# The accumulator of the fetched value rows in SBUF instead of two PSUM banks

## What is computed

```python
q = (xt @ w_query).reshape(t, 8, 2, 128)
s = einsum('thpd,hpkd->thpk', q, sub_keys)       # product keys
# top-16 per half, then top-16 of the 16 x 16 sums, for 8 heads:
# experts es (t, 128) out of 16384 and their softmax gates gs (t, 128)
u = expert_u[es]
vv = expert_v[es]                                # rows of 1024
a = gelu(einsum('tkd,td->tk', u, xs))
y = einsum('tk,tkd->td', gs * a, vv)
x = layer_norm(ALPHA * x + ga2 * y, ln2_g, ln2_b)
```

## Time and profile before

| | |
|---|---|
| median of 3 runs | 2309.18 us (2309.13 to 2312.66) |
| the profiled execution | 2312.7 us |
| its span | 2310.9 us |
| PE busy | 1959.6 us (85%) |
| DVE busy | 1613.4 us (70%) |
| POOL busy | 971.7 us (42%) |
| ACT busy | 196.6 us (9%) |
| DMA | 669.14 MB, mean 290 GB/s |

### The profile page before, as it was taken

The page is one execution under the profiler, slowest core; times in us unless marked ns, Lnnn a source line. Parts: engine busy times, 40 slices in busy tenths (PEclk is TensorE's granted clock), DMA queues, the critical chain, the costliest instruction groups (busy, mean ns, idle before and its releaser), DMA issues.

```text
span 2310.9 us, 22648 instructions
## 1 busy us (share of the span) xinstructions
PE 1959.6 (85%) x8018; PEld 1343.0 (58%) x8018; DVE 1613.4 (70%) x2879; ACT 196.6 (9%) x370; POOL 971.7 (42%) x1051
## 2 busy tenths in 40 slices
PE   3878799878899688999999999899999766999900
PEld 0557644355444247998889964347878766444400
DVE  0210476699678787899995897556565599776698
ACT  0020010134200001111100000000000000000000
POOL 7000026655455540145551026565555255655462
PEclk8889899967899898999997579999999755899955
DMA  9898648977799984269994039999999465899994
GB/s 290 301 319 250 236 138 310 314 246 237 267 372 332 365 309 175 73 229 347 338 359 149 1 145 363 356 409 409 409 410 409 153 216 188 336 409 409 410 410 184
DMA packets 227588, 669.14 MB, mean 290 GB/s; under 512 B 20476, under 2 KB 46204, under 8 KB 227356
## 3 DMA queue, kind: packets, MB, share of 16 engines
q0 software_dynamic: 114240, 410.27, 47.8%
q1 hardware_dynamic: 109504, 245.39, 29.4%
q10 hardware_dynamic: 3744, 12.14, 1.5%
HBM read 658.23 MB, written 7.39 MB: 288 GB/s over the span
## 4 chain that ended last, share of the span: by engine, by line
PE 44%; DVE 21%; DMA 17%; issue 12%; POOL 6%; ACT 0%; POOLq 0%; DVEq 0%; SPq 0%
PE psum L702 19%; PE psum L734 9%; DMA arena<-in_expert_v_dram,arena 9%; DVE psum L1381 7%; POOL arena L493 5%; DVE arena L1169 5%; PE psum L816 5%; PE psum L722 5%; DMA arena<-in_expert_u_dram,arena 3%; PE psum L573 2%; DMA arena<-in_w_ada_dram 2%; DMA arena<-in_w_in_dram 1%; DVE arena L1153 1%; DVE arena L1422 1%; DVE arena L1416 1%
## 5 line engine op out<-in xcount | busy, mean ns | idle before, releaser
L1169 DVE CUSTOM_DVE_ANT_0 arena<-arena 128x1024 f32<-128x1024 f32 x384 | 459.3, 1222 | 217.9 <-DMA arena<-in_expert_u_dram,arena 202.8
L1381 DVE SCALAR_TENSOR_TENSOR psum<-arena,psum 128x1024 f32<-128x1024 f32 x381 | 490.0, 1286 | 112.0 <-DMA arena<-in_expert_v_dram,arena 90.9
L493 POOL DMA_INDIRECT arena<-in_expert_u_dram,arena x384 | 470.6, 1226 | 171.3 <-issue 102.8
L734 PE MATMUL psum<-arena 128*128 128x512 f32 x1024 | 446.6, 599 | 10.0 <-DMA arena<-in_expert_v_dram 8.5
L493 POOL DMA_INDIRECT arena<-in_expert_v_dram,arena x384 | 381.9, 995 | 166.6 <-issue 90.3
L702 PE MATMUL psum<-arena 128*128 128x256 f32 x2048 | 445.0, 380 | 5.8 <-DMA arena<-in_expert_uT_dram 5.8
L702 PEld LDWEIGHTS psum<-arena 128*128 128x128 f32 x2048 | 390.3, 191 | 59.8 <-issue 6.6
L488 POOL COPY arena<-arena 128x4 uint32 x192 | 73.2, 381 | 692.5 <-DVE arena L1169 316.7
L734 PEld LDWEIGHTS psum<-arena 128*128 128x128 f32 x1024 | 196.8, 193 | 258.5 <-issue 247.3
L722 PE MATMUL psum<-arena 128*128 128x64 f32 x1024 | 218.4, 411 | 54.3 <-DVE arena L1422 52.9
L722 PEld LDWEIGHTS psum<-arena 128*128 128x128 f32 x1024 | 213.2, 319 | 59.9 <-issue 57.8
(11 more groups left out here) (152 smaller groups left out, 1591.0 us busy)
## 6 DMA issues: line engine op xcount, KB each, us to landing
arena<-in_expert_uT_dram SPq DMA_DIRECT2D x128, 512.0 KB
arena<-in_expert_v_dram SPq DMA_DIRECT2D x128, 512.0 KB
arena<-in_w_in_dram SPq DMA_DIRECT2D x16, 2048.0 KB
arena<-in_w_ada_dram SPq DMA_DIRECT2D x12, 2048.0 KB
arena<-in_w_query_dram SPq DMA_DIRECT2D x8, 2048.0 KB, 54.4
arena<-in_w_in_dram SPq DMA_DIRECT2D x16, 512.0 KB, 14.5
arena<-in_w_o_dram SPq DMA_DIRECT2D x4, 2048.0 KB
arena<-in_expert_u_dram,arena POOLq DMA_INDIRECT x384
```

Source lines behind the costliest of these rows:

```text
L493: pool.indirect_dma_start(slots[b], None, table[0], bass.IndirectOffsetOnAxis(ap=NUM[side][:, b:b + 1], axis=0)).then_inc(land, 16)
L734: mm = pe.matmul(bank(2 + 2 * d + hf), H[:, n % KEYHALF, d * P:(d + 1) * P], RINGS[load % RING][:, hf * HALF:(hf + 1) * HALF], start=n == ...
L1169: dve.tensor_tensor_reduce(UR[b], UR[b], U2B[e], 1.0, 0.0, ALU.mult, ALU.add, DOT[:, b:b + 1]).then_inc(u_free, 1)
L1381: dve.scalar_tensor_tensor(YS, row, weight, YS, ALU.mult, ALU.add).then_inc(v_free, 1)
```

## The change

The definition of YS as two PSUM banks goes, and YS becomes 1024 floats per partition of SBUF, taken from the region of small tensors. Nothing else is edited.

```diff
@@ -154,7 +154,6 @@
         def bank(b, n=1):
             return psum[:, b * HALF:(b + n) * HALF]
 
-        YS = bank(6, 2)
 
 
         def at(off, *shape):
@@ -223,6 +222,7 @@
         IDXF = keep(2 * PEER_HEADS * TOPK)
         EID = [keep(HK).bitcast(U32) for _ in range(2)]
         GATE, DOTS = [keep(HK) for _ in range(2)], [keep(HK) for _ in range(2)]
+        YS = keep(D)
         DGATE = {e: at(4 * P + P * d, HK) for d, e in enumerate(DENSE)}
         SPREAD = {e: keep(3, P) for e in DENSE}
```

## The result

| | before | after |
|---|---|---|
| median of the runs on the same chip | 2311.26 us | 2329.78 us |
| range of the runs | 2309.13 to 2312.71 us | 2319.25 to 2332.43 us |
| ratio after / before, with its 95% interval | | 1.0071 [1.0044, 1.0098] |
| profiled execution | 2312.7 us, span 2310.9 | 2332.0 us, span 2330.2 |

The change makes the kernel slower: the ratio is worth 0.0071 x 2311 = 16.4 us (10 to 23), against a forecast of +8.0. The two profiled executions lie 19.3 us apart.

The account below looks back on a forecast made before the run. No engine was taken to bound the whole span, so each stretch was judged by itself. The terms -2.1 - 1.3 + 12 + 0 + 2 - 2.6 = +8.0 us took 2309.2 to 2317.2 us; range 2298 to 2343 us.

Parts of the forecast that it names:

- Duration of a row: DVE's value rows L1381: with SBUF operands a dependent row saves 0.13 us, one before an independent instruction 0.05 us.
- Terms 1: Norm stage: three batches of six value rows between tiles each save 0.70 us, -2.1 us.
- 2 (gate half, -1.3): Second gate half: 31 rows save 0.05 us each, less 0.3 for meetings of gathers with L1169, -1.3 us.
- 6 (last 24 rows, -2.6): Last 24 rows: 23 x 0.13 saved, +0.4 for POOL's reads among them, -2.6 us.
- Term 3: Merge stage: DVE rows hold POOL's COPY and first gather, +7.4 over 11 groups, +4.6 over 13, together +12 us.
- Term 4: Row pairs: POOL may lose some 2 us on each of 16 groups, covered by DVE's wait; priced at 0.
- the cover: Before the second gate half: DVE's 34.6 us wait for PE hides POOL's losses; without it, up to +10 us.
- Term 5: Rows to 2249 us: DVE gains against POOL's held gathers, bounds -3.9 and +17, taken as +2 us.
- a lead is spent: Rows to 2249 us: POOL's 12-row lead over DVE partly lost between 2094 and 2200, most of it surviving.
- A: Rival, whole kernel: gathers run unblocked or DMA swallows the delay; -10.6 to -14.6 us, about 2297 us, chance 0.22.
- B: Rival: POOL's spacing copies DVE's, COPY on top; merge +30, end +17, total +41, 2350 us, chance 0.18.
- C: Rival: merge stage at +5 and the end at 0, total -1, about 2308 us, chance 0.22.

Follow-up runs that it names:

- tile 0 alone: Accumulator YS in SBUF for tile 0 only, in PSUM for tiles 1 and 2, against the kernel before: 1.0064 [1.0042, 1.0085], +14.7 us.
- Tiles 1 and 2 together: Accumulator YS in SBUF for tiles 1 and 2, in PSUM for tile 0, against the kernel before: 2308.27 us, 1.0018 [1.0006, 1.0031].
- tile 1 or tile 2 alone: Two kernels, YS in SBUF for only that tile, against the kernel before: tile 1 1.0003 [0.9993, 1.0012], tile 2 0.9990 [0.9980, 1.0000].

## Why the prediction was right or wrong

The direction, the place and the mechanism were right: slower, chiefly in the merge stage, because POOL's reads of row numbers are held by DVE's two SBUF inputs. The range held the time; the point was 12.6 us too low against the median of after. 2.1 of these come from the kernel before, which had 2311.3 in five runs where the forecast had 2309.2 from three; by the ratio the cost is 16.4 where 8.0 was forecast, twice as much.

**The step that failed is "Duration of a row".** It took L1304 (1.22 us, all operands in SBUF) as the row's duration with an SBUF accumulator, 0.13 us less for a dependent row, 0.05 for an independent one. L1304's scalar is a constant, L1381's a pointer to the weight, and the constant is what makes the duration 60 ns shorter. In spacing it makes 0.06 us, by the kernels with the constant; the other 0.07 of the 0.13 is a difference between a value row and L1304 that neither the place nor the scalar accounts for. In the changed kernel L1381 stayed at 1284 ns and its spacing at 1.39. The profile before held rows that pointed to the scalar, DVE's groups of L1117 (a pointer scalar and all operands in SBUF, 511 columns) and L1416 (another operation without a scalar, 512 columns), 65 ns apart:

```profile
L1416 DVE TENSOR_TENSOR arena<-arena 128x512 f32<-128x512 f32 x64 | 43.6, 681 | 0.3 <-DVE arena L1174 0.3
...
L1117 DVE SCALAR_TENSOR_TENSOR arena<-arena 128x511 f32<-128x511 f32 x4 | 2.7, 746 | 0.0
```

By term:

- Terms 1 (norm stage, -2.1), 2 (gate half, -1.3) and 6 (last 24 rows, -2.6) measured 0, 0 and -0.1. These 6.0 us are most of the miss: without them the same sum is +14.0, and the measured cost is 16.4 (10 to 23).
- Term 3 (merge stage, +12) measured +11.3 in the profile after; with tile 0 alone the stage is 13.7 us longer than before. Over the 11 groups it gave 0.65 us a group where 0.67 was worked out, but the parts differ, and that the size came out is partly luck. The COPYs grew by 5.9/11 = 0.54 us a group, as the term had it (1.26 instead of 0.19 in every second group). The gathers grew by 9.1/11 = 0.83, where the term had 0.3 on one gather in eight, 0.15 a group. And the term left out that POOL would wait less for its slots: 7.9/11 = 0.72 us a group, which took up nearly all of that. (The term's own parts, 1.07 and 0.3 less 0.13, make 1.24 us per two groups, not 1.35.)
- Term 4 (row pairs, 0): the stretch from the norm stage to the second gate half grew by 1.3 us, and DVE's wait for PE ahead of the gate half is 34.4 us where it was 34.6, so the cover held within that. Tiles 1 and 2 together cost 4 us by the runs, which their profile does not place.
- Term 5 (to tile 3's finish, +2) measured +5.7 in one profile and -0.1 in another. It worked with 6.4 us for POOL's group; measured are 6.95, in step with DVE. The idea that a lead is spent was right, and that it would mostly last; how large it is at the start differs between executions.

Of the rivals, **A** (the lock does not bite) falls: gathers went from 995 to 1196 ns, and the end of the merge stage is 11 us late. The kernel that reads PSUM and writes SBUF keeps its gathers at 987 ns, and its time does not change: where nothing is held, nothing is lost, and A's gains on DVE are not there either. **B** (POOL in step) is right on the mechanism at the end, 1.38 us from gather to gather and the COPY on top, but wrong on the price: the merge stage gave 11.3 and not 30, as half of the holds in its 11 groups came out of POOL's waits, and at the end the lead took it up in whole or in part. **C** (balance) needed the DVE gains that do not exist.

## What to carry to other kernels

Before taking one row as the duration of another, compare the kind of its scalar and what it waits for, and not only the places and shape of its operands: here the scalar was all of the difference in duration, and half of that in spacing. A running accumulator beside POOL's indirect gathers belongs in PSUM if all other operands lie in SBUF, because what counts is how many inputs DVE reads from SBUF; what POOL does between gathers (the small copy) is held too, and taking it out was worth 18 to 20 us, about what the change of place cost. Held gathers cost little where POOL had a lead (tile 1 or tile 2 alone: nothing that the runs show) and most where it had to wait for slots: count the gathers it is ahead by before pricing them. And price a hold against the idle time that it replaces.

## What the runs showed of the hardware

- A pointer scalar costs L1381 60 ns over a constant (1286 against 1227 ns in PSUM, 1284 against 1223 in SBUF). With the pointer, reading PSUM and writing SBUF takes 1278 ns, and the other way round 1294.
- L1378, one input times a pointer scalar, lasts 1285 ns when it writes PSUM and 751 ns when it writes SBUF (DVE's group in the profile after, below). It occurs three times, so it moves nothing here.

```profile
L1378 DVE TENSOR_SCALAR arena<-arena 128x1024 f32<-128x1024 f32 x3 | 2.3, 751 | 2.2 <-DMA arena<-in_expert_v_dram,arena 1.7 <-DVE arena L1174 0.5
```

- Beside back-to-back DVE rows with two SBUF inputs, POOL's gathers fall into step with them, 1.38 us apart instead of their own 1.24 (0.94 and 0.30 of idle time).
- Leaving out a copy of 0.18 us and its 0.80 us of wait in each group of four gathers gave 18 to 20 us, about half of it where POOL fetches u rows for tile 0. Why that part gained some 10 us was not tried apart.
